# A causal depthwise convolution recast for TensorE: rows of four shifts by 32 channels, three channel groups there and one on VectorE

## What is computed

```python
def causal_dwconv(u, w, b):
    """u: (B,T,C); w: (W,C); b: (C,). Causal depthwise conv over positions."""
    kern = w[:, None, :].astype(u.dtype)
    y = lax.conv_general_dilated(u, kern, window_strides=(1,), padding=[(CONV_WIDTH - 1, 0)],
                                 dimension_numbers=('NWC', 'WIO', 'NWC'), feature_group_count=CONV_CH)
    return y + b.astype(u.dtype)
...
    u = ca * jax.nn.sigmoid(cb)
    u = causal_dwconv(u, conv_w, conv_b)
    u = jax.nn.silu(layernorm(u, cn_w, cn_b))
```

## Time and profile before

| what | us |
|---|---|
| median of 3 runs (1208.49 to 1208.99) | 1208.9 |
| span of the profiled execution | 1206.2 |
| TensorE busy in it | 1192.1 |
| VectorE busy | 981.7 |
| ScalarE busy | 791.8 |
| GpSimd busy | 51.8 |

### The profile page before, as it was taken

The page is one execution under the profiler, slowest core; times in us unless marked ns, Lnnn a source line. Parts: engine busy times, 40 slices in busy tenths (PEclk is TensorE's granted clock), DMA queues, the critical chain, the costliest instruction groups (busy, mean ns, idle before and its releaser), DMA issues.

```text
span 1206.2 us, 16760 instructions
## 1 busy us (share of the span) xinstructions
PE 1192.1 (99%) x6775; PEld 1029.6 (85%) x6775; DVE 981.7 (81%) x940; ACT 791.8 (66%) x741; POOL 51.8 (4%) x77
## 2 busy tenths in 40 slices
PE   9999999999999999999999999999999999999997
PEld 8998999999899888888888888888888888888885
DVE  5998755445698979989979879879889989979987
ACT  6865644334566657687677768668668668767764
POOL 5000000000100000000000000000000000000000
PEclk9999999999999999999999999999999999999999
DMA  8942555556555259999999999999999999999990
GB/s 272 368 159 70 192 178 197 185 176 196 187 175 176 73 191 366 381 372 394 376 374 390 376 379 383 377 379 387 381 386 376 381 385 375 380 387 376 395 339 36
DMA packets 182572, 359.61 MB, mean 298 GB/s; under 512 B 9206, under 2 KB 68956, under 8 KB 182492
## 3 DMA queue, kind: packets, MB, share of 16 engines
q1 hardware_dynamic: 178300, 343.28, 79.3%
q0 software_dynamic: 4176, 15.21, 3.3%
q10 hardware_dynamic: 16, 0.00, 0.0%
HBM read 350.60 MB, written 7.86 MB: 297 GB/s over the span
## 4 chain that ended last, share of the span: by engine, by line
PE 94%; DVE 2%; issue 1%; SPq 1%; ACT 1%; DMA 0%; ACTq 0%; DVEq 0%
PE YB L2036 18%; PE WBS L2015 13%; PE WBS L2017 13%; PE WBS L2016 13%; PE YB L1653 6%; PE WBS L1580 5%; PE WBS L1582 4%; PE WBS L1581 4%; PE YB L2027 2%; PE WBS L1767 2%; PE WBS L1614 2%; PE YB L2051 2%; PE WBS L1615 2%; PE WBS L1616 2%; PE YB L1634 1%; PE YB L1797 1%
## 5 line engine op out<-in xcount | busy, mean ns | idle before, releaser
L929 DVE TENSOR_TENSOR w_lo<-raw,w_hi 128x2048 fp32r<-128x2048 f32 x319 | 716.4, 2288 | 85.5 <-ACT w_hi L578 85.2
L578 ACT ACTIVATE w_hi<-raw 128x2048 fp32r<-128x2048 f32 x324 | 598.5, 1915 | 11.0 <-DMA raw<-in_w_in 6.9
L2015 PE MATMUL WBS<-w_hi,t_hi 128*128 128x512 f32 x704 | 278.7, 396 | 0.6 <-DVE w_lo L929 0.5
L2017 PE MATMUL WBS<-w_hi,t_lo 128*128 128x512 f32 x704 | 274.8, 390 | 0.0
L2016 PE MATMUL WBS<-w_lo,t_hi 128*128 128x512 f32 x704 | 274.2, 389 | 0.0
L2015 PEld LDWEIGHTS WBS<-w_hi,t_hi 128*128 128x128 f32 x704 | 132.2, 188 | 29.6 <-issue 2.8
L2017 PEld LDWEIGHTS WBS<-w_hi,t_lo 128*128 128x128 f32 x704 | 132.2, 188 | 28.3
L2016 PEld LDWEIGHTS WBS<-w_lo,t_hi 128*128 128x128 f32 x704 | 132.3, 188 | 26.3
L1580 PE MATMUL WBS<-t_hi,w_lo 128*128 128x256 f32 x448 | 127.2, 284 | 0.0
L1582 PE MATMUL WBS<-t_lo,w_hi 128*128 128x256 f32 x448 | 126.8, 283 | 0.0
L1581 PE MATMUL WBS<-t_hi,w_hi 128*128 128x256 f32 x448 | 126.8, 283 | 0.0
(11 more groups left out here) (315 smaller groups left out, 1384.5 us busy)
## 6 DMA issues: line engine op xcount, KB each, us to landing
raw<-in_we_down SPq DMA_DIRECT2D x88, 1024.0 KB, 7.3
raw<-in_we_gate SPq DMA_DIRECT2D x80, 1024.0 KB, 7.0
raw<-in_we_up SPq DMA_DIRECT2D x80, 1024.0 KB, 6.9
raw<-in_w_in SPq DMA_DIRECT2D x19, 1024.0 KB, 5.6
raw<-in_wd_gate SPq DMA_DIRECT2D x11, 1024.0 KB, 5.3
raw<-in_wd_up SPq DMA_DIRECT2D x11, 1024.0 KB, 5.3
raw<-in_wd_down SPq DMA_DIRECT2D x11, 1024.0 KB, 4.9
raw<-in_w_out SPq DMA_DIRECT2D x8, 1024.0 KB, 11.2
```

Of the source, the lines that this page charges most:

```text
L578: act.activation(w_hi[:, hi_slot(n, item), :], raw[slot][:], ACT.Copy).then_inc(hi_ready, 1)
L929: dve.tensor_tensor(w_lo[slot][:], raw[slot][:], w_hi[:, hi_slot(n, item), :].bitcast(F32), ALU.subtract).then_inc(lo_ready, 1)
L2015: pe.matmul(bank, xs_hi[:, k0 + k, :], hi[:, k, :], start=start, stop=False)
L2017: ins = pe.matmul(bank, xs_lo[:, k0 + k, :], hi[:, k, :], start=False, stop=stop)
```

## The change

Group 0 alone stays on VectorE: even taps go into `acc`, odd ones into `acc_odd`, and one addition joins the two chains. Groups 1, 2 and 3 go to TensorE. Each block of 32 channels is laid out four times, each copy on 32 partitions of its own and shifted by one token more (`shifted`). One matmul then has 128 rows (four shifts by 32 channels) and 64 columns (32 channels by two taps that are 16 apart), and four of them (QS) cover a block. A product in `PE_CONV` is a pair of such matmuls, for two blocks, whose outputs are partitions 0 to 63 and 64 to 127. A layer has 24 products, 8 for each group.

GpSimd issues 16 transfers at the start (rows of taps, two layers by four by two, each 12 rows of 3 or 4 pieces of 128 bytes), ahead of its masks, and 32 in each mixer that fill `shifted`: 16 after the first half of the convolution's input is there, 16 (of two groups each) after the second. `turn_params` waits for the first 16 and turns four tiles, before it turned three. `make_pairs`, `pairs` and `diagonals` go; VectorE makes each group's operands in one operation of 1024 elements (`conv_weights`), that of layer 1's first group already in the dense stage. `place` and `add_ahead` take four operations of 32 partitions per group, where two of 64 partitions did for a group's placing and two for both groups' adding.

In TensorE's order levels 2 and 3 go into the middle of CA1 and CB1, levels 4, 5 and 6 between the four halves of G0 and G1, levels 7 and 8 behind G1; then 8 products, the heads, 11 products, the transposes, 5 products. ScalarE's order of layer 0 and 1 follows (exponentials earlier, group 0 placed before the root's table is loaded, 1 and 2 after the heads are split). VectorE's order in layer 0 is in the diff; in layer 1 it has 12 steps instead of 6 before `decayed(0)`, none between the read-outs, and 2 and 1 around the splitting. The tap rows that come through SyncE are halved, and the memory that is set aside for GpSimd's transfer descriptors is a quarter of the default (`dynamic_dma_scratch_size=4096`).

```diff
-    DIAGS = 6
+    APART = 16
+    QS = APART // 4
+    ON_PE = [[1, 2, 3], [1, 2, 3]]
...
-        cu = sm("cu", [P, CT, PAD + T])
-        c_sq = cu[:].rearrange("p c t -> p (c t)")[:, 0:CT * T]
+        cu = sm("cu", [P, 2, PAD + T])
...
+        shifted = sm("shifted", [P, 12, T + APART - 4])
+        shift_w = sm("shift_w", [P, QS, 4, 2, 32])
...
-        acc_sum = diag[:, 0:4, :].rearrange("p (g a) j -> p g (a j)", g=2)
+        acc_sum = shifted[:].rearrange("p c t -> p (c t)")[:, CT * T:(CT + 2) * T].rearrange("p (g t) -> p g t", g=2)
 
         xT = [Difs[:].rearrange("p a k t -> p (a k t)"), att[:].rearrange("p r a i -> p (r a i)")]
...
 
 
-        DVE_CONV = [(c, w) for w in range(TAPS) for c in (0, 1)]
-        APART = 16
...
+        def conv_operand(i):
+
+            if i == 0:
+                return shift_w[:]
+            return t_mem[:, i - 1, HEADS * T:(HEADS + CT) * T].rearrange("p (q b v j) -> p q b v j", q=QS, b=4, v=2)
+
+        def conv_bank(l, i):
+
+            return WB[[3, 2, 3][i] if len(ON_PE[l]) == 3 else [3, 2][i]]
...
+            step(pool.memset(shift_rows[:], 0.0))
+            for l in range(L):
+                for q in range(QS):
+                    for ahead in range(2):
+                        w0 = APART - 1 + 4 * q - APART * ahead
+                        first = max(0, -w0)
+                        r0 = 24 * q + ahead
+                        pool.dma_start(shift_rows[r0:r0 + 23:2, l, 32 * first:P].rearrange("p (s c) -> p s c", c=32),
+                                       conv_w[l, w0 + first:w0 + 4, P:CH].rearrange("s (b c) -> b s c", c=32)).then_inc(shift_rows_ready, 16)
...
+                pool.memset(shifted[:, :, 0:APART - 1], 0.0).then_inc(shift_pads, 1)
...
+                pool.wait_ge(shift_pads, l + 1)
+                if ON_PE[l][0] == 1:
+                    pool.wait_ge(cu_ready, 2 * l + 1)
+                    for b in range(4):
+                        for s in range(4):
+                            n = T - 3 + s
+                            pool.dma_start(shifted[32 * s:32 * (s + 1), b, APART - 1 - s:],
+                                           cu[32 * b:32 * (b + 1), 1, PAD:PAD + n]).then_inc(shifted_ready[0], 16)
+                pool.wait_ge(cu_ready, 2 * (l + 1))
+                for b in range(4):
+                    for s in range(4):
+                        n = T - 3 + s
+                        pool.dma_start(shifted[32 * s:32 * (s + 1), 4 + b:12:4, APART - 1 - s:],
+                                       acc[32 * b:32 * (b + 1), 2:4, 0:n]).then_inc(shifted_ready[1], 16)
...
+                def place(i):
+
+                    act.wait_ge(conv_grouped, GROUPS_BEFORE[l] + i + 1)
+                    c = ON_PE[l][i]
+                    for h_ in range(2):
+                        for j in range(2):
+                            rows = slice(64 * h_ + 32 * j, 64 * h_ + 32 * (j + 1))
+                            act.activation(acc[rows, c, :], conv_bank(l, i)[64 * j:64 * j + 32, T * h_:T * (h_ + 1)], ACT.Identity,
+                                           bias=pv[rows, l, PV_CB + c:PV_CB + c + 1]).then_inc(conv_placed, 1)
 
...
+            def conv_weights(l, i):
...
+                    after_unit(number_of(l, "G1"))
+                shape = [P, QS, 8, 32]
+                some = taps_x[:, l, :, 8 * (ON_PE[l][i] - 1):8 * ON_PE[l][i]]
+                dve.tensor_tensor(conv_operand(i).rearrange("p q b v j -> p q (b v) j"),
+                                  ident4[:].unsqueeze(1).unsqueeze(1).broadcast_to(shape),
+                                  some.unsqueeze(3).broadcast_to(shape), ALU.mult).then_inc(shift_w_ready, 1)
+
...
+                def add_ahead(i):
+
+                    c = ON_PE[l][i]
+                    for h_ in range(2):
+                        for j in range(2):
+                            dve.wait_ge(conv_placed, 4 * (GROUPS_BEFORE[l] + i) + 2 * h_ + j + 1)
+                            rows = slice(64 * h_ + 32 * j, 64 * h_ + 32 * (j + 1))
+                            part = acc[rows, c, APART:T]
+                            dve.tensor_tensor(part, part, conv_bank(l, i)[64 * j + 32:64 * j + 64, T * h_:T * (h_ + 1) - APART],
+                                              ALU.add).then_inc(conv_added, 1)
+
...
+                def sum_groups(g):
+
+                    ready = len(ON_PE[l]) if g else len(ON_PE[l]) - 2
+                    if ready:
+                        dve.wait_ge(conv_added, 4 * (GROUPS_BEFORE[l] + ready))
+                    if g == 0:
+                        for chain in range(2):
+                            dve.wait_ge(conv_step[chain], STEPS_BEFORE[chain][l + 1])
+                        if ON_PE[l][0] == 1:
+                            dve.tensor_tensor(acc[:, 0, :], acc[:, 0, :], acc_odd[:], ALU.add).then_inc(odd_added, 1)
+                            dve.wait_ge(odd_added, FIRST_BEFORE[l] + 1)
+                        dve.wait_ge(conv_grouped, GROUPS_BEFORE[l + 1])
+                    dve.tensor_tensor(acc_sum[:, g], acc[:, 2 * g, :], acc[:, 2 * g + 1, :], ALU.add).then_inc(acc_summed, 1)
 
                 done = [0]
 
...
+                    conv(6)
+                    lo(b + 6)
+                    decayed(0)
+                    decayed(1)
+                    differences(2)
+                    differences(3)
+                    lo(b + 7)
+                    conv_weights(0, 0)
+                    decayed(2)
+                    differences(4)
+                    lo(b + 8)
+                    decayed(3)
+                    differences(5)
+                    lo(b + 9)
+                    conv(2)
+                    decayed(4)
+                    conv(14)
+                    conv_input(1)
+                    level_read_out(3)
+                    differences(6)
+                    lo(b + 10)
+                    decayed(5)
+                    level_read_out(4)
+                    differences(7)
+                    decayed(6)
+                    lo(b + 11)
+                    level_read_out(5)
+                    decayed(7)
+                    level_read_out(6)
+                    conv(3)
+                    conv_weights(0, 1)
+                    conv_weights(0, 2)
+                    level_read_out(7)
+                    level_read_out(8)
+                    conv(1)
+                    add_ahead(0)
+                    head_sums(0)
+                    head_sums(1)
+                    head_gates()
+                    conv(2)
+                    head_lo(0)
+                    head_lo(1)
+                    conv(3)
+                    add_ahead(1)
+                    sum_groups(0)
+                    add_ahead(2)
+                    sum_groups(1)
...
                 def conv(count):
 
-                    for c, w in PE_CONV[done[0]:done[0] + count]:
-                        n = done[0]
-                        if n < BY_SCALAR:
-                            pe.wait_ge(diag_ready, BY_SCALAR * l + n + 1)
-                            both = diag[:, n % DIAGS, :]
+                    for i, c, h_, q in PE_CONV[l][done[0]:done[0] + count]:
+                        if done[0] == 0:
+                            pe.wait_ge(v_ready, 2 * (l + 1))
+                        if done[0] % (2 * QS) == 0:
+                            if c == 1:
+                                pe.wait_ge(shifted_ready[0], 16 * 16 * (FIRST_BEFORE[l] + 1))
+                            else:
+                                pe.wait_ge(shifted_ready[1], 16 * 16 * (l + 1))
+                            pe.wait_ge(shift_w_ready, GROUPS_BEFORE[l] + i + 1)
+                            if i == 2:
+                                pe.wait_ge(conv_placed, 4 * (GROUPS_BEFORE[l] + 1))
+                                pe.wait_ge(conv_added, 4 * (GROUPS_BEFORE[l] + 1))
+                        for j in range(2):
+                            ins = pe.matmul(conv_bank(l, i)[64 * j:64 * (j + 1), T * h_:T * (h_ + 1)],
+                                            conv_operand(i)[:, q, 2 * h_ + j].rearrange("p v j -> p (v j)"),
+                                            shifted[:, 4 * (c - 1) + 2 * h_ + j, 4 * q:4 * q + T],
+                                            start=(q == 0), stop=(q == QS - 1))
+                        done[0] += 1
+                        if done[0] % (2 * QS) == 0:
+                            ins.then_inc(conv_grouped, 1)
...
                 level(6)
-                conv(3)
+                gates_tile(1, 1)
                 level(7)
-                conv(3)
...
-                for hd in range(HEADS):
-                    for t in range(TT):
-                        a = HEADS * t + hd
-                        c0 = T * (hd % 2) + P * t
-                        ins = pe.transpose(WB[hd // 2][:, c0:c0 + P], o_sq[:, DV * a:DV * (a + 1)], ident[:])
-                ins.then_inc(o_turned, 1)
...
                 pe.wait_ge(rows_ready, 16 * (6 * L + 1))
-                for l in range(L):
```

(24 more changed lines are left out.)

471 lines of the change are left out of this document (235 added, 236 removed).

## The result

After takes 1219.55 us (median of 4 runs, 1217.84 to 1220.77), before 1208.70 us (4 runs beside them): a ratio of 1.0091, 95% interval [1.0077, 1.0105]. I had forecast 1206.0 us with a range of 1202 to 1212. It is 10.85 us slower, and none of my rivals gave it. The profiled execution took 1217.84 us with a span of 1216.0 us, 9.8 over before's.

A forecast was written before the change was run, and what follows sets the result against it. TensorE, busy 1192.1 of 1206.2 us, was taken to bound the kernel, with VectorE deciding before the heads. Terms -1.2 - 1.9 + 0.2 = -2.9 us gave profile 1203.3, median 1206.0 us; range 1202.0 to 1212.0.

The forecast's parts named there:

- The sum -1.2 - 1.9 + 0.2: Whole kernel: net of layer 0's mixer, layer 1's mixer and one more parameter transpose at the start, -2.9 us.
- Nothing for these: Start and mixers: GpSimd's new transfers, and the operand made in the dense stage, were given no cost.
- Column halves overlap: TensorE's convolution products: matmuls on column halves run beside each other like row halves, 0.45 us a product.
- The first rival: Convolution products: column halves don't overlap, 0.90 us a product, 1226.5 us in all; chance 0.13.
- the second (0.57): Convolution products: column halves overlap only in part, 0.57 us a product, 1210.8 us in all; chance 0.09.
- Up to the heads' transposes: Each mixer's first part: heads at 86.4 against 88.54, transposes at 94.5, 2.3 us earlier.
- the fourth rival: Before the heads: VectorE is still what they wait for, gain halved or gone, 1208.5 us; chance 0.14.
- The tail: From transposes to second output unit: additions at 0.35 us, second unit 1.0 us late in layer 0, 0.3 in layer 1.
- hidden, with 3.2 to spare: Start: GpSimd's 16 transfers at 0.53 us an issue land by 13.0, before the parameters' transposes at 16.23.
- the third rival: Start: GpSimd's issues cost 1.09 us each and hold TensorE, a gap of 5.7 us, 1211.7 us; chance 0.12.

The follow-up runs named there:

- e5: The changed kernel with 96 unused bytes per partition behind ident4: 1211.13 us, ratio 1.0021 to before.
- e8: e5 with V0's second half ahead of the parameters' transposes and three reorderings on ScalarE and VectorE in both mixers: 1207.01 us, ratio 0.9988 to before.
- e13: The kernel before with 32 bytes left free ahead of its first tile, so every tile moves: ratio 1.0001 to before.
- e4: The kernel before with only eT_hi and eT_lo moved by 32 bytes: ratio 1.0041 to before.
- e10: e8 with SyncE's small row transfers issued after the third weight unit (CB0) instead of before it: ratio 0.9999 to before.
- e11: e10 with the first half of the output unit's remainder moved ahead of the heads' sums on VectorE, both mixers: ratio 0.9998 to before.
- e7: e5 with only layer 0's eight tap-row transfers, so layer 1's convolution uses wrong taps: 1210.09 us.

## Why the prediction was wrong

**The step that failed** is one I never made. I costed the operations that the edit changed and their order; I did not ask what else the smaller `taps`, the new `ident4` and the other tiles displace. The sum -1.2 - 1.9 + 0.2 has no term for the dense stage and none for the experts. There lay +1.2 us and +6.2. e5, with 96 bytes left free, has neither. The second step is "Nothing for these", my term for the new transfers and their issues: the start came 2.9 us later (below).

**Column halves overlap.** Eight products, the 32 records at 85.68 in after's chain, took 3.63 us: 0.454 each, as I took it from row halves. The first rival (0.90) and the second (0.57) are both out. The 0.57 came from the Trainium skill's page "TensorE: Matmul & The Clock Gate", "Part 3: Packing small matmuls — row/col tiling", whose figure is for three column tiles; two of 64 columns cost no more here than two row halves (0.448 by rows 2).

**Up to the heads' transposes** every term held. The eight products end, and the heads begin, at 85.68 + 3.63 = 89.31, that is 36.5 us behind level 0; I had 86.4 for a level 0 at 49.93, also 36.5. TensorE does not wait between the eight products and the heads. The transposes come 44.68 us behind level 0 in both layers, where before had 46.91: 2.2 earlier, 2.3 forecast. VectorE kept up, so the fourth rival is out.

**The tail** was mis-sized. From the transposes to the second output unit before took 11.8 us and after 13.9; I had allowed 1.1 more, it is 2.1. VectorE's rows of after:

```profile
99.38 1.41 DVE L1185 SCALAR_TENSOR_TENSOR t_lo<-WBS,pv,t_hi 128x512 fp32r<-128x512 f32 x2 [1.12 <-ACT t_hi L718]
...
102.00 1.71 DVE L1091 TENSOR_TENSOR acc<-acc,WBS 32x240 f32<-32x240 f32 x4
103.74 0.43 DVE L1103 TENSOR_TENSOR acc<-acc,acc_odd 128x256 f32<-128x256 f32 x1
104.20 0.42 DVE L1106 TENSOR_TENSOR shifted<-acc 128x256 f32<-128x256 f32 x1
104.66 1.71 DVE L1091 TENSOR_TENSOR acc<-acc,WBS 32x240 f32<-32x240 f32 x4
```

An addition costs 0.43 us, not the 0.35 that I worked out by columns between 0.27 and 0.64: 8 x 0.08 = 0.6. The join and the two sums, 0.44 each for 0.4, add 0.1. ScalarE's eight placings (3.89 us from 99.81, 0.49 each where I had 0.42) are ahead of the additions that need them: VectorE has no wait behind the split. So mixer 0 gained 0.1 instead of 1.2, mixer 1 1.0 instead of 1.9. e8 shows that another order more than makes up for the dearer additions: with it the gains are 1.8 and 2.1.

**The start** was "hidden, with 3.2 to spare". The issue price was right (16 in 8.90 us, 0.56 each), so the third rival, GpSimd's price, did not come. What I left out is that SyncE's transfers in the same function change too: 1.4 us more of issuing, and 1.0 more of landing. These 2.4 of the +2.9 us I take for the change's, since before's own start varies by 1.6 us from run to run.

**The sum** for the part that I did cost, -2.9 us, would have been +1.8 in the profile (start +2.9, mixers -1.1); the 0.5 at the very end I had not seen either. The median of after lies another 1 us further above its span than before's, where the clock may play in.

## What to carry to other kernels

An edit that changes a tile's size moves every tile behind it: compare the addresses of all stationary and streamed operands before and after, modulo 256, and leave a gap where the distance between partners changed. When matmuls in code that was not touched change by a few ns each, look there first; it is cheap to try (one unused tile). Here it was worth 8.4 us of the medians, and placing the tokens won 4.4 us in the kernel before. In a mixer whose tail is short operations on two engines, put each where its engine is idle in the trace before judging the change as a whole.

## What was not expected of the hardware

- The rate of an fp32r matmul (marked f32 in the trace, 128 x 128 stationary) hangs on the distance of the stationary from the streamed tile in memory, modulo 256 bytes. For 512 streamed columns: 227.9 ns from start to start at 0, 229.8 at 192, 233.0 to 234.3 at 32, 64, 128, 160 and 224; 96 was not tried. For 256 streamed columns 0 is not the best: 119.9 ns, 116.8 with the streamed tile 32 further and 118.2 with it 32 short; the units with stationary tokens 119.8, 118.3 (tokens 32 further) and 117.1 (32 short). So in both, the stationary tile 32 short of the streamed one is the best of the three. e13 and e4, with `eT_hi` at one and the same address and 227.9 and 233.9 ns, show that the stationary tile's address by itself does nothing. Why, and whether loading the stationary tile meets the stream in the same piece of memory, no run shows. The Trainium skill, page "SBUF — State Buffer", section "Operand start alignment", allows an operand at any multiple of its element's size; these runs agree, and add that it isn't free.
- Two fp32 matmuls of 64 columns on the two column halves of the array, 256 columns streamed, take 0.454 us a pair, where two on row halves take 0.448.
- A transfer whose source is the first half of each of 31 rows took SyncE 0.82 and 0.67 us to issue, where the 31 whole rows took 0.53 and 0.26, and the issue behind it 0.99 and 0.84 for 0.26 and 0.31. That the shape is the reason is not isolated.
- After a wait of TensorE at the start the granted clock can fall to 0.50 once it works again: in e5 after 2.35 us of waiting, and not in after, with 2.81 us, nor in e10's profile, with 2.34 us. It cost 1.5 us in e5. e11's profile has it too, from 22.4 us on. When the clock first rises differs too: the record of it begins at 7.48 us in after and at 11.88 in e7, whose V0 began 2.1 us later.
